# Recurrence weights' low part in other steps, the tail of retention reordered, product weights requested sooner, mixing tiles loaded in pairs

## What is computed

```python
h = rms_norm(x, in_norm_g)
q, k, v, g, xr, gr, m_ret, m_rnn = split(h @ w_in)              # 10240 columns
y_ret = (silu(g) * head_norm(retention(rot(q), rot(k), v))) @ w_ret_o   # 4 heads, chunks of 128
y_rnn = (rg_lru(conv4(xr)) * gelu(gr)) @ w_rnn_o
x = x + (sigmoid(m_ret) * y_ret + sigmoid(m_rnn) * y_rnn) @ w_out
x = x + conv_gated_mlp(rms_norm(x, ffn_norm_g))
out = rms_norm(x, final_norm_g)
```

## Time and profile before

| | |
|---|---|
| median of 3 runs | 2005.13 us (2004.74 to 2007.83) |
| profiled execution, its own time | 2004.68 us |
| its span in the trace | 2002.9 us |
| instructions | 24562 |
| mean granted clock of TensorE | 0.998 of full |
| PE busy | 1962.8 us (98%) |
| PE weight loads | 1637.5 us (82%) |
| DVE / ACT / POOL busy | 71% / 47% / 16% |
| HBM | 162 GB/s over the span |

### The profile page before, as it was taken

One profiled execution on the slowest core, in us unless ns is written; L12 is line 12 of the kernel. 1 busy time (PEld: TensorE's weight loads), 2 busy tenths in 40 slices (PEclk: granted clock), 3 DMA queues, 4 the chain that ended last, 5 costly groups with the idle time before them and its releaser, 6 DMA issues.

```text
span 2002.9 us, 24562 instructions
## 1 busy us (share of the span) xinstructions
PE 1962.8 (98%) x9208; PEld 1637.5 (82%) x9208; DVE 1427.7 (71%) x1627; ACT 935.3 (47%) x1182; POOL 318.9 (16%) x265
## 2 busy tenths in 40 slices
PE   8999999999999999999999999999999999999998
PEld 6888888888888888887878787898788888888887
DVE  7877877776755444667777657757988788776766
ACT  6443353343445555454554443346544544543335
POOL 2000000010481000066665003200000000000000
PEclk9999999999999999999999999999999999999999
DMA  6343554454696443465668455631222222156523
GB/s 257 123 161 137 183 189 149 161 180 155 228 324 256 158 158 126 152 206 172 187 183 261 164 199 177 212 127 66 103 84 84 79 76 97 64 188 234 202 99 131
DMA packets 222461, 325.07 MB, mean 162 GB/s; under 512 B 12080, under 2 KB 150704, under 8 KB 222128
## 3 DMA queue, kind: packets, MB, share of 16 engines
q1 hardware_dynamic: 196320, 231.79, 35.0%
q0 software_dynamic: 22608, 85.99, 11.0%
q10 hardware_dynamic: 3456, 6.29, 0.9%
HBM read 223.36 MB, written 100.66 MB: 162 GB/s over the span
## 4 chain that ended last, share of the span: by engine, by line
PE 75%; DVE 10%; DMA 4%; issue 3%; ACT 3%; POOL 3%; SPq 1%; ACTq 0%; DVEq 0%; POOLq 0%
PE ps L346 25%; PE ps L348 24%; PE ps L347 24%; DMA qkv<-scr_v 1%; DVE ws L329 1%; POOL tr L915 1%; POOL tr L919 1%; DMA gel<-scr 1%; POOL tr L917 1%; DMA raw<-w_ret_o 1%; DVE wx L2135 1%; SPq L589 0%; PE ps L1198 0%; DVE state L2426 0%; DVE mxf L2478 0%
## 5 line engine op out<-in xcount | busy, mean ns | idle before, releaser
L1480 ACT ACTIVATE wx<-raw 128x1024 fp32r<-128x1024 f32 (+1 forms) x152 | 137.5, 906 | 252.1 <-DVE raw L2111 129.4
L346 PE MATMUL ps<-xs,wx 128*128 128x512 f32 x612 | 239.0, 391 | 2.1 <-DVE xs L2565 1.6
L348 PE MATMUL ps<-xs,wx 128*128 128x512 f32 x612 | 238.2, 389 | 0.0
L347 PE MATMUL ps<-xs,wx 128*128 128x512 f32 x612 | 238.1, 389 | 0.0
L2135 DVE TENSOR_TENSOR wx<-raw,wx 128x1024 fp32r<-128x1024 f32 (+1 forms) x152 | 159.0, 1047 | 30.2 <-ACT wx L1480 30.0
L346 PE MATMUL ps<-sc,wx 128*128 128x512 f32 x448 | 174.3, 389 | 0.0
L347 PE MATMUL ps<-sc,wx 128*128 128x512 f32 x448 | 174.3, 389 | 0.0
L348 PE MATMUL ps<-sc,wx 128*128 128x512 f32 x448 | 174.3, 389 | 0.0
L1515 ACT ACTIVATE ub<-ps 128x512 f32<-128x512 f32 x112 | 66.9, 597 | 158.7 <-PE ps L348 156.0
L346 PEld LDWEIGHTS ps<-xs,wx 128*128 128x128 f32 x612 | 114.9, 188 | 28.6 <-issue 2.7
L348 PEld LDWEIGHTS ps<-xs,wx 128*128 128x128 f32 x612 | 114.9, 188 | 23.8
(11 more groups left out here) (289 smaller groups left out, 4842.0 us busy)
## 6 DMA issues: line engine op xcount, KB each, us to landing
raw<-w_in SPq DMA_DIRECT2D x80, 512.0 KB, 5.4
scr<-ost POOLq DMA_DIRECT2D x32, 1024.0 KB, 5.2
raw<-w_up SPq DMA_DIRECT2D x44, 512.0 KB, 4.1
tq<-w_down SPq DMA_DIRECT2D x88, 128.0 KB, 2.7
scr_t<-tq POOLq DMA_DIRECT2D x22, 512.0 KB, 3.2
scr_h<-vt POOLq DMA_DIRECT2D x11, 1024.0 KB, 4.3
tr<-w_ret_o SPq DMA_DIRECT2D x64, 128.0 KB, 4.2
scr_q<-tr POOLq DMA_DIRECT2D x16, 512.0 KB, 5.2
```

What stands on the lines that cost most here:

```text
L346: pe.matmul(out, w(HI), x(HI), start=first, stop=False, skip_group_check=True)
L347: pe.matmul(out, w(HI), x(LO), start=False, stop=False, skip_group_check=True)
L348: return pe.matmul(out, w(LO), x(HI), start=False, stop=last, skip_group_check=True)
L1480: act.activation(dst, src, ACT.Copy).then_inc(sem["f_hi"], 1)
```

## The change

- DVE makes the low part of block h + 1 of `w_rnn_o` at j = 5 (the first quarter) and j = 7 (the other three), each ahead of the state's update, in place of halves at j = 3 and 5 behind it.
- ACT makes evacuation 15 before it converts chunk 1, and PE's first unit waits for 15; the sixteenth is waited for by the first unit of job 1.
- In the tail DVE takes the statistics and coefficients of chunk 31 before the low parts of product chunk 1.
- SP requests the weights of product chunks 2 and 3 sooner, before y22's first and second part.
- The sums of product activations begin at chunk 4, not 3.
- `msg` and `mrb` have six slots, loads are of two tiles; three pairs are loaded by SP, behind chunks 10, 12 and 15, and five by ACT behind the conversions of tiles 1, 3, 5, 7 and 9. Tiles 4 to 7 are mixed a little later. (The entries of the table of shared semaphores follow.)

```diff
-    msg, e = at("msg", [P, 4, HALF], F32, C)
-    mrb, e = at("mrb", [P, 4, HALF], F32, e)
+    msg, e = at("msg", [P, 6, HALF], F32, C)
+    mrb, e = at("mrb", [P, 6, HALF], F32, e)
...
-    def mix_load(eng, n):
-        half, t = mix_at(n)
-        cols = slice(half * HALF, (half + 1) * HALF)
+    def mix_load(eng, g):
+
+        half, t = mix_at(2 * g)
+        cols, slots = slice(half * HALF, (half + 1) * HALF), slice(2 * (g % 3), 2 * (g % 3) + 2)
         for dst, src, row in ((msg, scr, ROW_MR), (mrb, scr_r, 0)):
-            eng.dma_start(dst[:, n % 4, :], src[row + t * P:row + (t + 1) * P, cols]).then_inc(sem[f"mx_in{n % 4}"], 16)
+            eng.dma_start(dst[:, slots, :], src[row + t * P:row + (t + 2) * P, cols].rearrange("(m p) c -> p m c", p=P)
+                          ).then_inc(sem[f"mx_in{g % 3}"], 16)
...
             stored_y(14)
+            reto_w(2)
             reto_y(1, 0, 1, 0, 2, "y22a")
+            y_store(30)
+            reto_w(3)
             reto_y(1, 0, 1, 2, 8, "y22b")
-            reto_w(2)
-            y_store(30)
+            y_store(31)
             sp_.wait_ge(blk[1], PAIR_RNNO + 3)
             reto_y(2, 0, 0, 0, 4, "y21a")
             reto_y(2, 0, 0, 4, 8, "y21b")
-            reto_w(3)
-            y_store(31)
...
-                if i == 18:
+                if i == 10:
                     for slot in range(2):
                         sp_.wait_ge(stored[slot], 16 * PAIR_OUT)
-                    for n in range(4):
-                        mix_load(sp_, n)
+                if i in MIX_AT:
+                    mix_load(sp_, MIX_AT.index(i))
...
                 if unit == 0:
                     pe.wait_ge(sem["ys_sp"], KT + 2)
+                    pe.wait_ge(sem["evac"], 15)
+                if n == 0 and job == 1 and k == 0:
                     pe.wait_ge(sem["evac"], 16)
...
             for r in range(2):
                 qk_hi(r)
                 v_hi(r)
-            for job in range(2, 4):
-                evac_job(LAST_PAIR, 1, job, ACT.Sigmoid, 8)
+                evac_job(LAST_PAIR, 1, 2 + r, ACT.Sigmoid, 8)
...
-                if n < 12:
-                    mix_load(act, n + 4)
-
-            MIXED_HI = {23: (0, 1), 24: (2, 3), 25: (4,), 26: (5, 6), 27: (7,)}
+                if n in (1, 3, 5, 7, 9):
+                    mix_load(act, n // 2 + 3)
+
+            MIXED_HI = {23: (0, 1), 24: (2, 3), 26: (4, 5), 27: (6, 7)}
...
+            RNNO_LO_AT = {5: (0, 1), 7: (1, 4)}
+
+            def rnno_w_lo(h, j):
+
+                pair, s_ = rnno_pair(h + 1)
+                q0, q1 = RNNO_LO_AT[j]
+                dve.wait_ge(*late_count("w_hi_a", h + 1))
+                if q1 > 2:
+                    dve.wait_ge(w_hi[s_], pair + 1)
+                cols = slice(q0 * BE // 4, q1 * BE // 4)
...
                     coefficients(r - 1)
+                if h < 3 and j in RNNO_LO_AT:
+                    rnno_w_lo(h, j)
                 if j < 7:
...
             gate(30)
+            stats(31)
+            coefficients(31)
             reto_w_lo(1)
             reto_y_lo(1)
-            stats(31)
-            coefficients(31)
             gate(31)
...
-            R_SUM_AT = {3: (0, 1), 4: (2, 3), 5: (4, 5), 6: (6,), 7: (7,), 8: (8,), 9: (9,), 10: (10,), 11: (11,),
+            R_SUM_AT = {4: (0, 1), 5: (2, 3), 6: (4, 5), 7: (6, 7), 8: (8,), 9: (9,), 10: (10,), 11: (11,),
```

More of the change, by code:

```diff
@@ L755, in _ @@
             reto_y(2, 0, 0, 4, 8, "y21b")
-            reto_w(3)
-            y_store(31)
             w_o = a["w_out"][0]
+            MIX_AT = (10, 12, 15)
             for i in range(4, R_CHUNKS):
@@ L970, in _ @@
                 half, t = mix_at(n)
-                pool.wait_ge(sem[f"mx_in{n % 4}"], 32 * (n // 4 + 1))
+                pool.wait_ge(sem[f"mx_in{n // 2 % 3}"], 32 * (n // 6 + 1))
                 pool.wait_ge(sem["acc"], mix_acc(n))
-                pool.tensor_tensor(msg[:, n % 4, :], msg[:, n % 4, :], yacc[:, t, half * HALF:(half + 1) * HALF],
+                pool.tensor_tensor(msg[:, n % 6, :], msg[:, n % 6, :], yacc[:, t, half * HALF:(half + 1) * HALF],
                                    ALU.mult).then_inc(sem["mx_mul"], 1)
@@ L2396, in reto_y_lo @@
                                   ALU.subtract).then_inc(late_sem("ry_lo"), 1)
+            RNNO_LO_AT = {5: (0, 1), 7: (1, 4)}
[6 more added lines that the diff above has]
+                cols = slice(q0 * BE // 4, q1 * BE // 4)
+                last = dve.tensor_tensor(ws[:, s_, LO, cols], raw[:, s_, cols], ws[:, s_, HI, cols].bitcast(F32), ALU.subtract)
+                if q1 == 4:
+                    last.then_inc(w_split[s_], 1)
             for r in range(32):
@@ L2431, in _ @@
                     last.then_inc(sem["t_done"], 1)
-                if j in (3, 5) and h < 3:
-                    s_ = rnno_pair(h + 1)[1]
-                    part = slice(0, BE // 2) if j == 3 else slice(BE // 2, BE)
-                    if j == 3:
-                        dve.wait_ge(*late_count("w_hi_a", h + 1))
-                    else:
-                        dve.wait_ge(w_hi[s_], rnno_pair(h + 1)[0] + 1)
-                    last = dve.tensor_tensor(ws[:, s_, LO, part], raw[:, s_, part], ws[:, s_, HI, part].bitcast(F32), ALU.subtract)
-                    if j == 5:
-                        last.then_inc(w_split[s_], 1)
             reto_w_lo(0)
@@ L2477, in mixed @@
                     dve.wait_ge(sem["mx_sp"], n - 1)
-                dve.tensor_tensor(mxf[:, n % 2, :], msg[:, n % 4, :], mrb[:, n % 4, :], ALU.add).then_inc(sem["mx_f"], 1)
+                dve.tensor_tensor(mxf[:, n % 2, :], msg[:, n % 6, :], mrb[:, n % 6, :], ALU.add).then_inc(sem["mx_f"], 1)
             def mixed_lo(n):
@@ L2502, in _ @@
                 elif i == 24:
+                    mixed_lo(1)
                     mixed(2)
-                    mixed_lo(1)
                     mixed(3)
@@ L2509, in _ @@
                     mixed_lo(3)
+                elif i == 26:
                     mixed(4)
-                elif i == 26:
                     mixed(5)
                     mixed_lo(4)
+                elif i == 27:
+                    mixed_lo(5)
                     mixed(6)
-                    mixed_lo(5)
-                elif i == 27:
                     mixed(7)
                     mixed_lo(6)
-                    mixed_lo(7)
             def reto_last(t):
@@ L2524, in reto_last @@
                 dve.tensor_tensor(yacc[:, t, HALF:], yacc[:, t, HALF:], ps[:, t, :], ALU.add).then_inc(sem["acc"], 1)
+            mixed_lo(7)
             mixed(8)
@@ L2538, in _ @@
             mixed_lo(11)
-            for n in range(13, 16):
-                mixed(n)
-                mixed_lo(n - 1)
+            mixed(13)
+            mixed_lo(12)
+            mixed(14)
+            mixed_lo(13)
+            mixed(15)
+            mixed_lo(14)
             mixed_lo(15)
```

## The result

The changed kernel takes 1990.68 us (median of 5 runs, 1989.3 to 1995.48); the kernel before, run beside it on the same chip, 2007.83 (2004.74 to 2008.91). The ratio is 0.9922, with a 95% interval of 0.9906 to 0.9938: by the ratio about 15.7 us less (the medians lie 17.2 apart), where 21.0 were forecast. Profiled execution against profiled execution it is 1990.17 against 2004.68, the spans 1988.1 and 2002.9.

What follows compares the result with a forecast made beforehand. TensorE, busy 98%, was taken as the bound, so only its waits and slow clock could be gained. Terms 9.9 + 0.5 + 1.1 + 3.5 + 5.3 + 0.7 = 21.0 gave 1984.1 us, range 1979.5 to 1991.

Steps and rivals of the forecast that it cites:

- Part 1: Recurrence: moving the weights' low part turns six steps of 9.08 us into 7.43, gaining 9.9 us, plus 0.5 at step 16.
- Just in time: Recurrence, step 5 to 6: the key low part ends about 904.4, where TensorE wants it at 904.5.
- The 0.5 at step 16: Recurrence: TensorE's wait for POOL at step 16 goes because its load comes earlier, gaining 0.5 us.
- Part 2: Start of the recurrence: TensorE's 0.99 us wait for the sixteenth evacuation goes with its edge, gaining 1.1 us.
- Part 3: Tail of retention: earlier statistics and weight requests let product chunk 3 start sooner, gaining 3.5 us, bounds 1 and 3.6.
- Chunk 4's weights in the tail: Example inside the nothing-gained rival: once a wait is removed, the load of product chunk 4's weights shows right behind; chance 0.03.
- Part 4: End of retention product and mixing: 10.1 us lost falls to 4.8, gaining 5.3, plus 0.7 at the third output block.
- No wait is as long as 3.46: End of the retention product: remaining waits stay shorter than the old 3.46 us one, so the clock does not fall.
- the port: Rival, recurrence: the quarter loses its turn to both of POOL's subtracts, 6 us lost, 1990 us; chance 0.18.
- the slower recurrence: Rival: DVE becomes the recurrence's bound and every step's pitch rises; at 7.93 us the kernel takes 2010; chance 0.03.
- The mixing: Rival: mixing stays the bound, its chain being order, not loads; part 4 gives 2 us, 1988; chance 0.14.
- nothing gained: Rival, whole kernel: each wait removed shows the next one right behind, 2004 us; chance 0.03.

Runs made afterwards that it cites:

- e1: The kernel before with only the new places of the recurrence weights' low part (a quarter at j = 5, three at j = 7): 1994.41 us, ratio 0.9940.
- e4: The changed kernel with the start undone (evacuations in their old places, first unit waits for 16): 1990.78 us, ratio 0.9916.
- e2: The kernel before with the tail alone (SP's new request order, DVE's last statistics first, sums from chunk 4): 2007.21 us, ratio 1.000.
- e5: The changed kernel with the weights of product chunk 4 requested ahead of y21's two parts: 1987.56 us, ratio 0.9902.
- e9: The changed kernel with GpSimd's product of tile 10 also waiting until the first output block is split: 1986.82 us, ratio 0.9899.
- e7: The changed kernel with chunk 4's weights requested ahead of y21 and the first w_out block split ahead of tiles 8 and 9: 1986.64 us, ratio 0.9899.
- e10: e7 with GpSimd's product of tile 10 held until the first output block is split: 1985.21 us, ratio 0.9893.
- e6: The changed kernel with the first w_out block converted ahead of tiles 6 and 7 and split ahead of tiles 8 and 9: 1989.32 us, ratio 0.9913.
- e8: The changed kernel with the recurrence block's low part in two halves (j = 5 and 7), not a quarter and three quarters: 1990.58 us, ratio 0.9920.
- e3: The changed kernel with the recurrence weights' move, the start and the tail undone, so mixing alone: 2003.71 us, ratio 0.9985.

## Why the prediction was right or wrong

The direction, the places and the largest term were right; a quarter of the sum did not come. By the traces the 21.0 us forecast became 14.8 of span.

**Part 1** (9.9 + 0.5): 9.9 in e1. Right, and for the reason given: in two of three heads the quarter gets its turn between two of POOL's subtracts. The Trainium skill (SBUF — State Buffer, Who interferes with whom) lets whoever issues first keep the shared port for its whole instruction; the trace agrees both ways: where DVE was first POOL's subtract took 1.60, and in the second head, where POOL was first, the quarter took 1.38. "Just in time" was too dark by 1.6 us in the first and third heads, where 1.7 us were in hand: the arithmetic took DVE's phase in step 5 from a trace in which step 3 had already delayed it. In the second head, with 0.27, it was right. The 0.5 at step 16 did not come. Its mechanism was wrong: the wait of 0.50 is gone, and the next step takes 0.4 more, for which no single wait shows, in every kernel with this part.

**Part 2** (1.1): step 0 fell by 0.6 us in the profile, and the first scores, which now wait for GpSimd, came 0.2 later. The old wait was 0.99 us in one execution and 2.20 in e4's, so the size taken from one row was one draw of it.

**Part 3** (3.5, bounds 1 to 3.6) is the first step that failed. The 3.5 came, 3.43 by the table, and 1.6 of it went again at the next chunk. The failed sentence is "The bytes are the same, so y21 and chunk 4's weights land near 1112 to 1115 as now". The bytes were the same, but not the time that the queues worked on them. Windows from the kernel before, two of 2 us at the end of retention (last two columns: DMA share, GB/s), and the same two of e2, where chunk 0 came 1.2 us later:

```profile
1094.00:1096.00 2.00, 2.00 (x11) 1.75 (x12) 1.28 (x2) 2.00 (x3) 0.00 (x0) 1.00 0.93 282
1096.00:1098.00 2.00, 2.00 (x11) 1.63 (x10) 1.76 (x4) 0.78 (x1) 0.74 (x1) 1.00 0.99 366
```

```profile
1094.00:1096.00 2.00, 1.70 (x10) 1.18 (x9) 1.34 (x2) 1.68 (x3) 0.00 (x0) 1.00 0.56 173
1096.00:1098.00 2.00, 2.00 (x11) 1.61 (x10) 1.83 (x2) 1.94 (x3) 0.00 (x0) 1.00 0.54 157
```

SP stood at the waits that the early requests brought with them, and (282 + 366 - 173 - 157) x 2 us = 636 KB less were moved, 1.6 us at 400 GB/s (1.3 with the shift of 1.2 us taken out). From 1102 to 1106 the rate was 337 and 269 GB/s where it had been 397 and 403, another microsecond; there the DMA engines were busy (share 1.03 and 1.01), and why they moved less is not shown. So in e2 the last of these loads, chunk 4's weights, came at 1118.7 and not at 1115.2 as before, and TensorE lost 2.3 us. I had moved SP's waits for low part 2 and for the gate ahead of y21 in the text, and charged nothing for them. "Chunk 4's weights in the tail" stood among the rivals, at 0.03 and joined to every other wait: the right place with the wrong price. The idle queues alone don't make the loss: in e5 they idle too (share 0.41 from 1082 to 1084), and with the order changed it is gone. The Trainium skill (DMA: Bandwidth & Descriptors, Queues, rings and completion order) says that each DMA engine takes descriptors in the order of its ring. The trace agrees: 11.8 us for 512 KB with y21 ahead, 6.6 with y21 behind.

**Part 4** (5.3 + 0.7) is the second; it gave 3.1 ahead of the projection and took 0.6 behind it. The losses by chunk were forecast at 0.3, 0.1, 1.7, 1.1, 0.1 and 1.5, and came as 0.45, 0.65, 1.49, 1.05, 0.25 and 3.08. Five were right within 0.6. The sixth was mis-sized, 3.08 for 1.5: I counted ACT's second conversion ahead of the block's, but not POOL's pair of products beside DVE's sums and low parts, 1.1 us for each pair. e9 takes away this collision alone, and the loss falls to 1.98; e7 takes away the order alone, with both pairs still slow, and it falls to 1.89; both, in e10, leave 0.66.

"No wait is as long as 3.46, so no fall of the clock" failed: it fell behind 2.81 and, in e2, behind 2.15 and 1.87. The 0.7 of the third output block did come, as e6 to e9 show (95.7 to 95.9 against 96.58), but the fall of the clock cost 1.5 in the same stretch (97.21 against e8's 95.73 behind the same wait).

The errors add up: 0.9 in the recurrence with its start, 0.2 before it, 1.8 in the tail, 2.2 ahead of the projection, 1.3 behind it, less 0.1 at the end, 6.2 in all but for rounding. Of the **rivals** neither the port (keys never waited over 0.2 us) nor the slower recurrence (the longer steps take 7.43 to 7.47 but for 7.56 and 7.59 at steps 13 and 14 and 7.99 at step 16) held. The mixing did not hold as told, since POOL took tiles 0 to 5 in one run of 10.67 us without a wait for a load; but "the chain is order, not loads" was half right: 7.0 of the 10.1 us stayed, and part 4's net of 2.5 is nearer to that rival's 2 than to the 6.0 forecast. The time lay near the upper end of the range for two losses just behind the places that were mended; only "nothing gained" had named one of them.

## What to carry over

Ask of each place that is mended which item is due next there, and whether its request stands behind megabytes that nobody needs yet: the small urgent load goes ahead of the large ones. A request moved forward takes its wait with it, and every load behind it in the queue pays for that. Where DVE and GpSimd work side by side and one of them is on the way to TensorE, a wait that holds the other back can be worth as much as an earlier start (1.1 and 1.2 us here), but it moves the collision, and the next consumer has to be looked at.

## What the runs showed of the hardware

A wait costs TensorE twice once the clock falls behind it, and the length of the wait does not decide that alone. In the stages from the recurrence on, in all twelve traces, the granted clock fell behind 3.83, 2.15 and 1.87 us (e2), 3.46, 3.28 (e5), 2.81 (after and e3), 2.80 and 2.20 (e4) and 2.42 (e1); behind none of 1.77 us or less did it fall. But it stayed full behind 2.88 in the kernel before (at 1257.41) and behind 2.82 in e8. TensorE's row and a window (clock third from the end) of the shortest wait with a fall, in e2, and of e8:

```profile
1257.94 0.47 PE L346 MATMUL ps<-ysr,wsr 128*128 128x512 f32 x1 [1.87 <-DVE ysr L2395]
...
1259.00:1261.00 2.00, 2.00 (x7) 1.59 (x6) 1.91 (x4) 1.17 (x2) 0.00 (x0) 0.54 1.09 380
```

```profile
1247.28 0.39 PE L346 MATMUL ps<-ws,mix 128*128 128x256 f32 x1 [2.82 <-DVE ws L329]
...
1248.00:1250.00 2.00, 2.00 (x19) 2.00 (x18) 2.00 (x4) 0.03 (x1) 0.00 (x0) 1.00 0.96 350
```

What is different in those two was not tried and stays open. Each of these is one execution. For planning, here a wait of 1.9 us or more had to be priced at its length and up to 1.7 us more.
